# A two-block transformer on one core: own inputs for recurrence pair three, four attention gate places, another K order in the first output tiles, ten modulation gate tiles there

## What is computed

```
mod = silu(c) @ w_ada + b_ada            # shift, scale, gate: 3 x 2048
h = rms(x) * (1 + scale) + shift
a_q, a_k, a_v, a_z, g_q, g_f, g_i, g_z = split(h @ w_in)
att = chunk_attention(a_q, a_k, a_v) * silu(a_z)      # 8 heads of 128
hg  = rms(hgrn2(g_q, g_f, g_i)) * silu(g_z)           # 8 heads of 128
x = x + gate * (concat(att, hg) @ w_out)
```

## Time and profile before

| what | value |
| --- | --- |
| median of three executions | 1596.85 us |
| the profiled execution's own span | 1599.0 us |
| TensorE busy by the page | 98% of the span |
| VectorE, ScalarE, GpSimd busy | 72%, 54%, 9% |
| mean granted TensorE clock | 0.994 |
| h103 begins, h104 begins | 327.0 us, 346.9 us |
| h112 begins | 392.6 us |
| h144 begins, h152 begins | 506.4 us, 531.6 us |

### The profile page before, as it was taken

The page is one execution under the profiler, slowest core; times in us unless marked ns, Lnnn a source line. Parts: engine busy times, 40 slices in busy tenths (PEclk is TensorE's granted clock), DMA queues, the critical chain, the costliest instruction groups (busy, mean ns, idle before and its releaser), DMA issues.

```text
span 1599.0 us, 24289 instructions
## 1 busy us (share of the span) xinstructions
PE 1573.0 (98%) x9650; PEld 1400.7 (88%) x9650; DVE 1154.1 (72%) x1696; ACT 862.4 (54%) x1321; POOL 151.6 (9%) x164
## 2 busy tenths in 40 slices
PE   8998999989999999999999999999999999999999
PEld 6787889988999999988799888888888888888887
DVE  6797867877778886759778777777777777455544
ACT  6855546767665555655556454544444444444442
POOL 0000000321221220034213000000000000000000
PEclk9999999999999999999999999999999999999999
DMA  9999975533457774343244545555455454555552
GB/s 373 369 343 349 365 285 209 188 114 121 180 189 267 285 272 179 132 158 132 97 144 178 189 170 199 184 186 210 172 197 191 179 211 175 205 199 185 198 196 105
DMA packets 47825, 331.02 MB, mean 207 GB/s; under 512 B 5281, under 2 KB 6689, under 8 KB 8417
## 3 DMA queue, kind: packets, MB, share of 16 engines
q1 hardware_dynamic: 45184, 312.20, 53.5%
q0 software_dynamic: 2240, 17.04, 2.8%
q10 hardware_dynamic: 290, 0.25, 0.1%
HBM read 327.37 MB, written 2.10 MB: 206 GB/s over the span
## 4 chain that ended last, share of the span: by engine, by line
PE 89%; DVE 5%; DMA 3%; ACT 2%; issue 1%; POOL 0%; SPq 0%; ACTq 0%; DVEq 0%; POOLq 0%
PE ps L1173 20%; PE ps L1174 11%; PE ps L1169 9%; PE ps L1170 8%; PE ps L1171 8%; PE ps L1228 5%; PE ps L1227 5%; PE ps L1226 5%; PE ps L1216 4%; PE ps L1217 3%; PE ps L1218 3%; DVE wl L1916 2%; DMA raw<-in_wts 1%; DMA xs<-in_xN 1%; PE ps L1384 1%; PE ps L1351 1%
## 5 line engine op out<-in xcount | busy, mean ns | idle before, releaser
L1916 DVE TENSOR_TENSOR wl<-raw,wh 128x1024 fp32r<-128x1024 f32 x512 | 626.2, 1236 | 282.4 <-ACT wh L1519 281.9
L1519 ACT ACTIVATE wh<-raw 128x1024 fp32r<-128x1024 f32 x512 | 531.3, 1054 | 377.2 <-PE ps L1228 130.6
L1173 PE MATMUL ps<-hA,wh 128*128 128x512 f32 x1408 | 488.7, 390 | 0.0
L1174 PE MATMUL ps<-hA,wl 128*128 128x256 f32 x1408 | 397.0, 282 | 0.0
L1173 PEld LDWEIGHTS ps<-hA,wh 128*128 128x128 f32 x1408 | 264.2, 188 | 55.3
L1174 PEld LDWEIGHTS ps<-hA,wl 128*128 128x128 f32 x1408 | 266.1, 189 | 0.0
L1169 PE MATMUL ps<-hA,wh 128*128 128x256 f32 x752 | 219.5, 292 | 0.0
L1170 PE MATMUL ps<-hA,wh 128*128 128x256 f32 x752 | 211.7, 282 | 0.0
L1171 PE MATMUL ps<-hA,wl 128*128 128x256 f32 x752 | 211.7, 282 | 0.0
L1169 PE MATMUL ps<-hB,wh 128*128 128x256 f32 x576 | 164.4, 285 | 0.8 <-DVE work L2362 0.4
L1170 PE MATMUL ps<-hB,wh 128*128 128x256 f32 x576 | 161.1, 280 | 0.0
(11 more groups left out here) (303 smaller groups left out, 2077.9 us busy)
## 6 DMA issues: line engine op xcount, KB each, us to landing
raw<-in_wts SPq DMA_DIRECT2D x256, 1024.0 KB, 4.8
raw<-in_ada SPq DMA_DIRECT2D x36, 1024.0 KB, 6.1
side<-in_ada POOLq DMA_DIRECT2D x12, 1024.0 KB, 8.5
work<-in_memN SPq DMA_DIRECT2D x2, 1024.0 KB, 8.9
xs<-in_xN POOLq DMA_DIRECT2D x1, 2048.0 KB, 20.6
xs<-in_xT POOLq DMA_DIRECT2D x2, 1024.0 KB, 7.8
out_rows<-xs SPq DMA_DIRECT2D x8, 256.0 KB, 2.4
wp<-in_dt SPq DMA_DIRECT2D x8, 128.0 KB, 2.7
```

What stands on the lines that cost most here:

```text
L1173: e.matmul(ps[bank][:, :], w1, hl, start=first, stop=False)
L1174: i = e.matmul(ps[bank][:, T:2 * T], w2, hl[:, 0:T], start=False, stop=last)
L1519: e.activation(wh[:, h % WS, :], raw[:, n % RAW, part * HALF:(part + 1) * HALF], ACT.Copy).then_inc(s_hi)
L1916: e.tensor_tensor(wl[:, h % WS, :], src, wh[:, h % WS, :].bitcast(F32), ALU.subtract).then_inc(s_lo)
```

## The change

- **Recurrence inputs.** A third set of `fin`, `qin`, `zin` lies in the memory of K tiles 12 to 14 of `hB2`. `INPUT_SET = (1, 0, 2, 1)` gives pair 0 set 1, pair 1 set 0, pair 2 the new set, pair 3 set 1 again. f, q, z of pair 2 wait for no pair; those of pair 3 wait for pair 0 in place of pair 1. `kk` and the decay tables still have two sets: the sigmoid of pair 2 and 3 waits for pair 0 and 1 (`rec_head`).
- **Attention gates.** `zt` has four places: set 0 of the recurrence inputs (pair 1's) for az 0 to 2, one old place for az 3. The order now waits ahead of az 0 for pair 1, and ahead of az 3 for heads 0 to 3. The waits for gates 0 and 1 are gone.
- **Output line.** `OUT_STEPS` replaces `OUT_PARTS`: tiles 0 to 3 over K 8 to 11, then 0 and 2, then 12 and 13; tiles 4 and 5 over those eight; all six over 4, 6, 7; then 14, 15; then 1, 3, 5. The waits ahead of the line go into it: pairs 0 and 1 ahead of block 0, gates 0 and 1 at block 8, splits 0 and 2 at 16, pair 2 at 24, heads 4 to 7, the first load of `x` and gates 2 and 3 at 32, splits 4, 6, 7 at 48. Pair 3 stays at block 64.
- **Gate tiles.** Those with az 1 and az 3 and those at j = 4 and 5 go: six stand in the mix stage, four in the output line (ahead of its entries 2 to 5), six at tiles 6 to 11 as before.

```diff
+INPUT_SET = (1, 0, 2, 1)
 OUT_FIRST = 6
-OUT_PARTS = (tuple(range(8, 14)), (0, 2, 4, 6, 7), (14, 15), (1, 3, 5))
+OUT_STEPS = ((range(0, 4), (8, 9, 10, 11)), (range(0, 4), (0, 2)), (range(0, 4), (12, 13)), (range(4, 6), (8, 9, 10, 11, 12, 13, 0, 2)),
+             (range(0, 6), (4, 6, 7)), (range(0, 6), (14, 15)), (range(0, 6), (1, 3, 5)))
+OUT_LINE = tuple((j, kt) for tiles, kts in OUT_STEPS for j in tiles for kt in kts)
-GATES_WITH = {("q", 0), ("q", 1), ("z", 1), ("q", 2), ("az", 1), ("q", 3), ("z", 3), ("az", 3)}
-GATES_AT = range(4, 12)
+GATES_WITH = {("q", 0), ("q", 1), ("z", 1), ("q", 2), ("q", 3), ("z", 3)}
+GATES_LINE = range(2, 6)
+GATES_AT = range(6, 12)
...
         if j == OUT_FIRST - 1:
+            line = [("w_out", kt, (128 * i,)) for i, kt in OUT_LINE]
+            for i in range(OUT_FIRST):
+                if i in GATES_LINE:
+                    ada(2, gates.pop(0))
+                out.append(("s", "w_out", line[16 * i:16 * i + 16]))
...
+    def rec_head(p):
+        while p >= 2 and ("rt", p - 2) not in o.done:
+            yield
+        yield from stages(("rf", p), REC_HEAD)
...
     for kind, n in MIX:
-        if kind != "az" and n >= 2:
-            o.until(("rt", n - 2))
+        if kind != "az" and n == 3:
+            o.until(("rt", 0))
         if kind == "az":
             if n == 0:
+                o.until(("rt", 1))
+            if n == 3:
                 o.until(*[("att", h) for h in range(4)])
-            if n >= 2:
-                o.until(("gate", n - 2))
...
-            o.add(5, ("rf", n), stages(("rf", n), REC_HEAD))
+            o.add(5, ("rf", n), rec_head(n))
...
-    o.until(*[("att", h) for h in range(4, 8)])
-    o.beat("xload", 0)
...
-    o.until(*[("rt", n) for n in range(3)])
-    o.until(*[("gate", m) for m in range(4)])
-    for i, h in enumerate(OUT_PARTS[1]):
-        o.add(i % 2, ("gs", h), stages(("gs", h), ("hi", "lo")))
+    o.until(("rt", 0), ("rt", 1))
     for i in range(0, 16 * OUT_FIRST, 8):
+        if i == 8:
+            o.until(("gate", 0), ("gate", 1))
+            split_gates((5, 0), (5, 2))
+        if i == 16:
+            o.until(("gs", 0), ("gs", 2))
+        if i == 24:
+            o.until(("rt", 2))
         if i == 32:
-            o.until(*[("gs", h) for h in OUT_PARTS[1]])
+            o.until(*[("att", h) for h in range(4, 8)])
+            o.beat("xload", 0)
+            o.until(("gate", 2), ("gate", 3))
+            split_gates((0, 4), (1, 6), (0, 7))
+        if i == 48:
+            o.until(("gs", 4), ("gs", 6), ("gs", 7))
         if i == 64:
             o.until(("rt", 3))
...
+        third = nc.alloc_sbuf_tensor_at("third", [P, 3, 512], F32, offset=hB_off + 32 + 12 * 2048)
...
+        fin, zin, qin = ([(pair[:, 0, :], pair[:, 1, :], third[:, i, :])[n] for n in INPUT_SET] for i, pair in enumerate((fin2, zin2, qin2)))
-        zt = [av[:, 0, i, :] for i in range(2)]
+        zt = [fin2[:, 0, :], qin2[:, 0, :], zin2[:, 0, :], av[:, 0, 0, :]]
...
                 if k == "sigmoid":
                     e.wait_ge(*after(("f", 2 * pr + 1), "act", "ev"))
+                    if pr >= 2:
+                        e.wait_ge(*after(("rt", pr - 2), "dve", "lo"))
...
-                    if pr >= 2:
-                        e.wait_ge(*after(("rt", pr - 2), "dve", "lo"))
+                    if pr == 3:
+                        e.wait_ge(*after(("rt", 0), "dve", "lo"))
```

More of the change, by code:

```diff
@@ L142, in plan @@
             ada(2, gates.pop(0))
-    early, ends, late, last = [], [], [], []
     for j in range(KT):
@@ L146, in plan @@
             ada(2, gates.pop(0))
[L147 to L153, removed]
+        if j >= OUT_FIRST:
+            t = s_tile("w_out", (128 * j,))
             out.append(("s", "w_out", t[8:] + t[:8]))
         if j == OUT_FIRST - 1:
-            line = [b for part in (early, ends, late, last) for t in part for b in t]
-            out += [("s", "w_out", line[16 * i:16 * i + 16]) for i in range(OUT_FIRST)]
+            line = [("w_out", kt, (128 * i,)) for i, kt in OUT_LINE]
[3 more added lines that the diff above has]
+                out.append(("s", "w_out", line[16 * i:16 * i + 16]))
     kv, qu = "w_kv_up_2", "w_q_up_2"
@@ L664, in order, with split_gates @@
     o.in_half = o.half
-    o.until(*[("att", h) for h in range(4, 8)])
-    o.beat("xload", 0)
     first, rest = list(range(8, 16)), list(range(8))
     banks = [o.gemm_bank() for _ in range(4)] + [4, 5]
[L670 to L673, removed]
     for j in range(OUT_FIRST):
         o.take(("wo", j), banks[j])
-    o.until(*[("rt", n) for n in range(3)])
-    o.until(*[("gate", m) for m in range(4)])
-    for i, h in enumerate(OUT_PARTS[1]):
-        o.add(i % 2, ("gs", h), stages(("gs", h), ("hi", "lo")))
-    for i in range(0, 16 * OUT_FIRST, 8):
-        if i == 32:
-            o.until(*[("gs", h) for h in OUT_PARTS[1]])
+    line = [(("wo", j), banks[j], kt, kt == 8, kt == 5) for j, kt in OUT_LINE]
+    def split_gates(*heads):
+        for lane, h in heads:
+            o.add(lane, ("gs", h), stages(("gs", h), ("hi", "lo")))
+    o.until(("rt", 0), ("rt", 1))
+    for i in range(0, 16 * OUT_FIRST, 8):
+        if i == 8:
[5 more added lines that the diff above has]
+            o.until(("rt", 2))
+        if i == 32:
+            o.until(*[("att", h) for h in range(4, 8)])
[4 more added lines that the diff above has]
+            o.until(("gs", 4), ("gs", 6), ("gs", 7))
         if i == 64:
             o.until(("rt", 3))
-            for h in (1, 3, 5):
-                o.add(h % 3, ("gs", h), stages(("gs", h), ("hi", "lo")))
+            split_gates((1, 1), (0, 3), (2, 5))
         if i == 72:
@@ L965, in program @@
         a1 = 0
-        fin, a1 = carve(a1, 2, 512, of=early)
-        qin, a1 = carve(a1, 2, 512, of=early)
-        zin, a1 = carve(a1, 2, 512, of=early)
+        fin2, a1 = carve(a1, 2, 512, of=early)
+        qin2, a1 = carve(a1, 2, 512, of=early)
+        zin2, a1 = carve(a1, 2, 512, of=early)
+        fin, zin, qin = ([(pair[:, 0, :], pair[:, 1, :], third[:, i, :])[n] for n in INPUT_SET] for i, pair in enumerate((fin2, zin2, qin2)))
         kk, a1 = carve(a1, 512, of=early)
@@ L1374, in rec_end @@
                     e.wait_ge(*after(t, "act", "sq"))
[L1375 removed]
+                    e.matmul(ps[6][:, :], ones[:], fin[t[1]], start=True, stop=True).then_inc(mark(t, "pe", "ss"))
             def softmax(t, k, bank, pairs, causal, v, B):
@@ L2091, in rec_end @@
                 pr = t[1]
-                f, r, z = (x[:, pr % 2, :] for x in (fin, qin, zin))
+                f, r, z = (x[pr] for x in (fin, qin, zin))
                 if k == "r1":
```

29 lines of the change are left out of this document (14 added, 15 removed).

## The result

The changed kernel is slower by 0.6%. Its median is 1607.73 us (1605.14 to 1611.12, four runs), that of the kernel before, run beside it, 1599.01 us (1596.31 to 1601.55, four runs): ratio 1.0059, 95% interval 1.0042 to 1.0077. The prediction was 1588.8, range 1581 to 1600. The profiled executions differ by 6.2 us of span; up to h103, and from h156 to the end, the two take the same time within 1.0 us.

A forecast was written before the change was run, and what follows sets the result against it. TensorE was taken to set the pace, with the four-pair recurrence as second chain. 11.1 us won at h152, less 2 for gate tiles and 1 behind h152, gave 8.1: 1596.85 - 8.1 = 1588.8 us, range 1581 to 1600.

The forecast's parts named there:

- The stretch at h104 goes: Mix stage: own inputs for pair 2 remove the stretch without weight blocks at h104; pair 2's f and q run there.
- z comes earlier, 22.2 becomes 6.2: Between pair 2's pv and pair 3's f1: the link falls from 22.2 to 6.2 us, worth 16 us to the chain.
- Each pass becomes 48.5, like those of pairs 2 and 3.: Recurrence, f1 to pv: every pass takes 48.5 us without the stretches, putting pair 3's f1 at 458.5, its sum at 509.5.
- the 17.7 us: h103 to h152: the most that steady feeding of TensorE gives back, half clock included; h152 would then begin at 513.9.
- Tail of pair 3: Ahead of h152: square to product takes 11 us from the sum at 509.5; h152 begins at 520.5, 11.1 us earlier.
- Other K order: Output line: new block order with waits spread; no cost, up to a few us if the attention lanes don't keep up.
- Gate tiles in the line: Four gate tiles in h144 to h151 overload VectorE and delay steps of pair 3's tail; 2 us charged, 0 to 5.
- Behind h152: After h152, up to 578.0: VectorE arrives with less slack; 1 us charged, 0 to 2.
- `HOLD`, 0 to 3 us: Unchanged table of fixed holds, written for other neighbours: tasks may meet TensorE too early; 0 to 3 us, only in the range.
- D: Rival, chance 0.12: VectorE bounds the line, four gate tiles add 9.9 us ahead of pair 3's tail; slower, about 1602.
- C: Rival, chance 0.23: the chain slips two to three us a pass, h152 at 526 to 529; won 1 to 4, about 1594.
- E: Rival, chance 0.05: another wait, heads 4 to 7 at block 32 or pair 0 at h112, replaces the stretches; 1597.

The follow-up runs named there:

- e5: Changed kernel, stages from f of pair 2 to the line's end allowed 0.5 us early, all lanes despite engines up to 4.5 us behind; ratio 1.0028.
- e17: e16 with recurrence stages allowed up to 0.5 us ahead of their due time, from f of pair 2 to the line's end; ratio 1.0019.
- e12: Changed kernel with scores, softmax and product with v of all eight heads left out, output wrong; ratio 0.9978 to the kernel before.
- e2: Changed kernel without the fixed holds of the recurrence tasks (rec, rf, rt); ratio 1.0066 to the kernel before.
- e4: Kernel before with only the new K order of the output line and its waits in the line; ratio 1.0006.
- e1: Changed kernel with its gate tiles back where the kernel before had them; ratio 1.0063 to the kernel before.
- e15: e10 with the gate tiles back where the kernel before had them; ratio 1.0005 to the kernel before.
- e10: Changed kernel without the fixed holds of rec, rf, rt, att, gate and gs; ratio 1.0011 to the kernel before.
- e16: e10 with the line's four gate tiles ahead of its first four tiles; ratio 0.9989 to the kernel before.
- e9: Kernel before without the fixed holds of rec, rf, rt, att, gate and gs; ratio 1.0000 to the kernel before.

## Why the prediction was wrong, step by step

- *"The stretch at h104 goes", the wait at h112 is little.* Right: 14.4 of 17.5 us won there.
- *z comes earlier, 22.2 becomes 6.2.* Right: 4.2 us, from pair 2's pv at 474.78 to pair 3's f1 at 478.99.
- ***"Each pass becomes 48.5, like those of pairs 2 and 3."* This is the step that failed.** They became 55.3, 56.2 and 59.6, so pair 3's f1 was 20.5 us late. The 48.5 were read from two passes of 48.4 and 48.9 us that held 12 and 14 halves of weight blocks; the three of the kernel after hold 15, 15 and 17. So the order set the stages wider apart, with more weight blocks between them; written denser, passes take 49.5 to 51.2 us (e5) or 47.0 to 49.7 (e17). Without the heads they take 51.0 to 51.9 (e12), 4 to 8 us less. My bounds were 41 and 51.5, and the trace of before excluded nothing above 51.5: "three more us" was no bound from a row.
- *The second fault is deeper, and the forecast gain hangs on it: that with such passes TensorE goes on at full pace, so that 11.1 of the 17.7 us come back.* e17 has passes as short as assumed and no gain, and e2's chain is 10.7 us earlier at pair 3's f1 and wins nothing. TensorE meets stages before they are ready, or weight and head splits behind them. In h103 to h156 the losses sum to 19.0 us or more in each of the sixteen orders of the full work, before and after among them, wherever the waits stand. That no order can do better isn't shown.
- *Tail of pair 3: square to product 9 to 11 us, h152 at 520.5.* Its start was late by 10 us, and the order put it between weights again: sum to low part 16.7 us, h152's first matmul at 531.12, and its first block that needs pair 3 at 536.44. What TensorE loses there, 6.5 us, is about what the prediction let it lose (520.5 - 513.9 = 6.6), but by chance, some 16 us later than forecast. Of the 13.4 us that it loses before, in h144 to h147, the sum had 2, for the gate tiles.
- *Other K order: "no cost", up to a few us.* Alone it is (e4, 2.3 us at h145). With gate tiles and the stages of pairs 2 and 3 on VectorE the split of heads 0 and 2, needed one half after it is written, costs 7.7 us at h145 and h146. I had looked at when the heads are ready, not at what VectorE has queued ahead of their low part.
- *Gate tiles in the line, 2 us (0 to 5).* Their mechanism was as feared (2.75 and 2.29 us ahead of an urgent low part, VectorE 10.22 of 10.26), but no other place of them wins more than 0.2%: e1 as after, e15 1.0005 against e10's 1.0011, e16 0.9989. VectorE was not full over the line: 37.87 of the 46.70 us from h144 to h152 (81%), where "over 95%" was the sign; it was full where it mattered, in the 10.26 us ahead of the split.
- *Behind h152, 1 us.* h156 to the end takes the same time in both.
- *`HOLD`, 0 to 3 us.* Mis-sized, and left out of the sum: it costs about 0.5%, 7.7 us (1.0059 against 1.0011), most of the slowdown. With the holds of rec, rf and rt alone gone nothing is won (e2), so those of the heads, gates and splits take part; which one weighs most wasn't tried. The rest of the miss is the gain that didn't come: 8.1 us forecast, and without holds 1.0011.
- *Rivals.* D came nearest (gate product ahead of the tail, "about 1602", decided by a sum of pair 3 later than 512: it was 519.65), and its sign was right. Its mechanism is seen at h152, but it isn't the whole: one gate tile and a half of weights stand ahead of the low part, 2.85 us in place of 9.9. C's sign is there too (f1 of pair 3 behind 465), with slips of 6.8 to 11.1 us a pass where it had two to three. E's sign is there as well, a stretch ahead of h148: 506.7 to 518.7 holds no weight block, ended by heads 4 to 7 and pair 3 at block 32, and without the holds E's outcome, nothing won, is what e10 measures. It had 0.05. None of the three priced the table of holds. D's chance of 0.12 took the slip of the chain and the queue on VectorE for separate mishaps; here they came together.

What stays open: the cause of the slowdown is shown (e9, e10), that of the missing gain only in part. That passes between blocks can't be both short and free of waits rests on orders of one kind, the same rule with other numbers; an order that ranks stages by what VectorE and ScalarE have queued wasn't tried. Nor was a later place for the blocks that need heads 0 and 2: the wait ahead of h146 stands in every version with the new K order, e4's too, and in e17 h145 to h147 lose 10.0 of its 21.8 us.

## What to carry to other kernels

When a stall vanishes, ask which serial chain ran at its fastest inside it, and cost that chain at its slow pace, with a bound above the slowest pass seen, before any gain is counted. When waits only change place from one order to the next and their sum stays, as here, shorten the work that is waited for (here two levels, worth 4.7 us more than their instructions in the changed kernel) before the waits are moved again. A table of hand-set delays must be dropped or made anew with a change to the order. And the low part of a split, on a queue that is worked off in order, is as late as all that is written ahead of it.

## What the runs showed of the hardware

- Waits of TensorE of 4.21 and 4.46 us in the line were followed by the lower level of the granted clock for 4.6 to 6 us more (497.56 to 503.4, 536.44 to 541.0), a matmul of 256 columns taking 0.41 in place of 0.28 us. Such a wait cost about half as much again: 6.5 us for 4.46 at h152.
- A gate tile took VectorE 2.28 to 2.29 us in most places, but 2.75 at 489.66 and 3.12 at 380.77 (kernel after) and 2.71 at 470.86 (kernel before). GpSimd was at work beside all three, for 0.60, 3.05 and 2.64 us. That alone doesn't decide: at 500.36 (after) it was at work for 2.06 us of a gate tile's 2.28, and at 541.40 (before) for all of its 2.29. What slows those three wasn't tested.
